# An FFN's gate and up by seven half-token products of block sums instead of eight, in a one-core Conformer-style block

## The reference

```python
def swiglu(h, w_gate, w_up, w_down):
    return (jax.nn.silu(h @ w_gate) * (h @ w_up)) @ w_down

x = x + 0.5 * swiglu(rms_norm(x, ffn1_norm), ffn1_w_gate, ffn1_w_up, ffn1_w_down)
h = rms_norm(x, mix_norm)
proj = h @ w_in                        # 1024 x 4624
...                                    # SSD scan of 16 heads, pooling over 4 groups
x = x + concatenate([y_ssd, y_pool]) @ w_out
x = x + 0.5 * swiglu(rms_norm(x, ffn2_norm), ffn2_w_gate, ffn2_w_up, ffn2_w_down)
out = rms_norm(x, final_norm)
```

## Time and profile before

| | us |
|---|---|
| median of 3 runs | 1042.38 |
| lowest, highest | 1042.3, 1042.4 |
| the profiled execution, device time | 1042.32 |
| its span in the trace | 1040.6 |
| busy: TensorE, VectorE, ScalarE, GpSimd | 1031.2, 559.6, 380.4, 179.1 |

### The profile page before, as it was taken

How to read it: one execution, slowest core, us unless ns; L and a number is a source line. 1 busy time by engine, 2 the same in 40 slices (tenths; PEclk the granted TensorE clock), 3 DMA queues, 4 the chain that set the end, 5 groups by cost and what they waited for, 6 DMA issues and landing times.

```text
span 1040.6 us, 13577 instructions
## 1 busy us (share of the span) xinstructions
PE 1031.2 (99%) x4798; PEld 847.3 (81%) x4798; DVE 559.6 (54%) x686; ACT 380.4 (37%) x489; POOL 179.1 (17%) x166
## 2 busy tenths in 40 slices
PE   9999999999999999999999999999999999999997
PEld 7888888888888878878787888888888888888887
DVE  5544444444344468786799795554444444433432
ACT  6433223322333337652234753432333223332332
POOL 1110110101001032221063451110101101101100
PEclk9999999999999999999999999999999999999998
DMA  6533323322333343222222233333333332233222
GB/s 184 150 113 101 101 86 95 101 83 68 99 98 96 101 124 100 82 81 70 73 81 81 62 101 101 101 101 90 92 101 101 96 87 89 79 109 95 86 68 81
DMA packets 188873, 99.09 MB, mean 95 GB/s; under 512 B 3780, under 2 KB 188200, under 8 KB 188840
## 3 DMA queue, kind: packets, MB, share of 16 engines
q1 hardware_dynamic: 188168, 97.60, 32.3%
q10 hardware_dynamic: 672, 1.05, 0.3%
HBM read 96.54 MB, written 2.10 MB: 95 GB/s over the span
## 4 chain that ended last, share of the span: by engine, by line
PE 96%; DVE 3%; issue 1%; ACT 1%; POOL 0%; ACTq 0%; POOLq 0%
PE bank L1150 29%; PE bank L1152 29%; PE bank L1151 29%; PE bank L1222 1%; PE bank L1216 1%; PE bank L1219 1%; PE bank L1471 1%; PE bank L1284 0%; PE bank L1306 0%; PE bank L1472 0%; PE bank L1473 0%; PE bank L1274 0%; DVE w_lo_part L743 0%; DVE ebuf L903 0%; PE bank L1190 0%
## 5 line engine op out<-in xcount | busy, mean ns | idle before, releaser
L1150 PE MATMUL bank<-xghi,w_hi_part 128*128 128x512 f32 x960 | 377.4, 393 | 0.0
L1152 PE MATMUL bank<-xghi,w_lo_part 128*128 128x512 f32 x960 | 373.8, 389 | 0.0
L1151 PE MATMUL bank<-xglo,w_hi_part 128*128 128x512 f32 x960 | 373.6, 389 | 0.0
L743 DVE TENSOR_TENSOR w_lo_part<-w_raw,w_hi_part 128x1024 fp32r<-128x1024 f32 x194 | 253.9, 1309 | 192.8 <-ACT w_hi_part L498 187.5
L498 ACT ACTIVATE w_hi_part<-w_raw 128x1024 fp32r<-128x1024 f32 x194 | 203.8, 1051 | 196.2 <-PE bank L1152 194.7
L1150 PEld LDWEIGHTS bank<-xghi,w_hi_part 128*128 128x128 f32 x960 | 180.2, 188 | 39.9 <-issue 2.8
L1151 PEld LDWEIGHTS bank<-xglo,w_hi_part 128*128 128x128 f32 x960 | 180.3, 188 | 38.4 <-issue 1.2
L1152 PEld LDWEIGHTS bank<-xghi,w_lo_part 128*128 128x128 f32 x960 | 180.2, 188 | 37.5
L1150 PE MATMUL bank<-acthi,w_hi_part 128*128 128x512 f32 x330 | 130.5, 396 | 0.0
L410 POOL TENSOR_TENSOR gate_buf<-gate_buf,rstd 128x512 f32<-128x512 f32 x44 | 57.1, 1298 | 424.5 <-ACT gate_buf L521 424.5
L1152 PE MATMUL bank<-acthi,w_lo_part 128*128 128x512 f32 x330 | 129.4, 392 | 0.0
(11 more groups left out here) (223 smaller groups left out, 805.0 us busy)
## 6 DMA issues: line engine op xcount, KB each, us to landing
w_raw<-in_ffn_w_gate SPq DMA_DIRECT2D x42, 512.0 KB, 3.8
w_raw<-in_ffn_w_up SPq DMA_DIRECT2D x42, 512.0 KB, 3.8
w_raw<-in_w_in SPq DMA_DIRECT2D x29, 512.0 KB, 3.8
w_raw<-in_ffn_w_down SPq DMA_DIRECT2D x32, 384.0 KB, 3.2
w_raw<-in_ffn_w_down SPq DMA_DIRECT2D x32, 320.0 KB, 3.0
w_raw<-in_w_out SPq DMA_DIRECT2D x16, 512.0 KB, 3.6
out<-xtok SPq DMA_DIRECT2D x4, 512.0 KB, 3.4
xload<-in_x SPq DMA_DIRECT2D x3, 512.0 KB, 7.0
```

The lines of the kernel that those rows point to most:

```text
L743: dve.tensor_tensor(wlo[:, slot(m)], raw[:, slot(m)], whi[:, slot(m)].bitcast(F32), ALU.subtract).then_inc(w_lo, 1)
L1150: pe.matmul(bank, w, h, start=first and n == 0, stop=False)
L1151: pe.matmul(bank, w, l, start=False, stop=False)
L1152: mm = pe.matmul(bank, wl, h, start=False, stop=last and n == blocks - 1)
```

## The change

Two hidden tiles of gate and up are taken together as a quad. With k for the two halves of the 1024 input channels, f for the two tiles, and the 512 tokens in two halves, gate and up are each a 2 x 2 by 2 x 2 block product. Instead of its eight block products the kernel makes seven, of sums of blocks (`A11`, `SUM1`, `SUM2`, `A12`, `SUM3`, `SUM4`, `A22`); each has 4 input blocks, gate and up, three matmuls: 24 matmuls of 256 columns. Some accumulate onto an earlier product in the same bank, the rest is added by VectorE (`gather`) after ScalarE has copied a product out of PSUM.

- Sums of weights: three by VectorE, one by GpSimd per quad. There are 7 conversions per quad where there were 4, all of 1024 elements.
- Sums of x (`combine`): four 256-token combinations for each of the 4 channel pairs, split into `thi` and `tlo`, once per FFN; in FFN1 in the steps of direct tiles 2 and 3, in FFN2 in the last four out-projection units.
- Direct, as before: tiles 0 to 3 of FFN1, tiles 0 and 1 of FFN2. So 9 and 10 quads.
- Each FFN runs in three groups of 8, 8 and 6 tiles; after each group all 8 output tiles get that group's part of down. `acthi`, `actlo` hold 8 tiles instead of 22. The first two down items of a group begin with all tiles but the last two.
- Up is not scaled by `rstd` any more; half of `rstd` is multiplied onto the down result (`down_scaled`), and a second VectorE instruction adds it to x.
- Eight raw buffers instead of four within FFNs; the loops are written out.

```diff
-DOWN = (6, 6, 5, 5)
+RAW = 8
+KH = UB // 2
+GROUP_TILES = (8, 8, 6)
+DIRECT_TILES = (4, 2)
+PARTS = 7
+A11, SUM1, SUM2, A12, SUM3, SUM4, A22 = range(PARTS)
...
 @blk.sync
+                if FREE[key]:
+                    sp.wait_ge(w_lo, FREE[key])
+                if key[0] == 1 and slot >= RING:
+                    sp.wait_ge(unit_done, M_FFN2)
...
 @blk.gpsimd
+            def third_sum(q):
+                pool.wait_ge(sum_ready[1], q + 1)
+                pool.tensor_tensor(weight(q, SUM3), weight(q, A11), weight(q, SUM3), ALU.add).then_inc(sum_ready[3], 1)
+            def scale_gate(q, i, h, done, ready):
+                pool.wait_ge(done, q + 1)
+                gate = post[:, q % 2, i, 0:HALF]
+                pool.tensor_tensor(gate, gate, rstd[:, half(h)], ALU.mult).then_inc(ready, 1)
             def gates(f):
+                        if not quad.chained:
+                            third_sum(q)
+                        scale_gate(q, 0, 0, c11_done, r11_ready)
+                        if not quad.last:
+                            third_sum(q + 1)
+                        scale_gate(q, 1, 1, c22_done, r22_ready)
+                        scale_gate(q, 2, 1, c12_done, r12_ready)
...
 @blk.scalar
+            def ffn(f, last):
+                for r, it in enumerate(items):
+                    if it.kind == "product" and it.part == SUM1:
+                        copy_product(q, A11, 0, q % 2, p1_read, act0_ready)
+                    if it.kind == "product" and it.part == SUM2:
+                        copy_product(q, SUM1, 1, 2, p5_read, act22_ready)
+                    if it.kind == "product" and it.part == A12:
+                        copy_product(q, SUM2, 2, q % 2, u2_read, act0_ready)
+                    if chained and it.part == SUM1:
+                        silu_odd(q - 1)
+                    if before is not None and before.kind == "direct":
+                        direct_post(f, before)
+                    if converted <= n + 3 < M_FFN2 + len(FFN2):
+                        convert(n + 3)
+                    if chained and it.part == A11:
+                        silu_even(q - 1)
+                    if chained and it.part == SUM2:
+                        split_act(q - 1, 0)
+                    if chained and it.part == SUM3:
+                        split_act(q - 1, 1)
+                    if f == 0 and it.kind == "direct" and it.raw >= RING:
+                        halves_of_x(0, it.raw - RING, R_N1)
+                        combination_hi(0, it.raw - RING)
+                    if it.kind == "down" and it.d == 0:
+                        silu_even(q)
+                        silu_odd(q)
+                        split_act(q, 0)
+                        split_act(q, 1)
+                    if it.kind == "down" and it.group == 2 and it.d:
+                        last(it.d - 1)
...
+            for d in range(DK):
+                square(2, d, d % 2, xT[:, cols(d)])
+                norm_hi(2, d, R_N2)
+                if d >= KH:
+                    halves_of_x(1, d - KH, R_N2)
+                    combination_hi(1, d - KH)
+                convert(M + U_OUTS + d + RING)
...
 @blk.vector
+            def combine(f, j, gain):
+                term(0, low[:, 0:HALF], g0, b12[:, j, :], ALU.subtract)
+                term(2, high[:, HALF:S], g4, b12[:, j, :], ALU.subtract)
+                dve.wait_ge(t_own, c + 1)
+                term(1, high[:, HALF:S], neg4, t32[:, j, 0, :], ALU.subtract)
+                dve.wait_ge(t_own, c + 3)
+                term(3, high[:, 0:HALF], neg4, t32[:, j, 1, :], ALU.subtract)
+            def combine_low(f, j):
+                dve.wait_ge(t_hi, KH * f + j + 1)
+                dve.tensor_tensor(tlo[:, :, j, :], t32[:, j, :, :], thi[:, :, j, :].bitcast(F32),
+                                  ALU.subtract).then_inc(t_lo, 1)
+            def first_sum(q):
+                dve.tensor_tensor(weight(q, SUM1), weight(q, SUM3), weight(q, A22), ALU.add).then_inc(sum_ready[1], 1)
+            def gather(q, part, i, bank, read, ready):
+                dve.wait_ge(unit_done, QUADS[q].base + part + 1)
+                dve.wait_ge(read, q + 1)
+                c = post[:, q % 2, i, :]
+                dve.tensor_tensor(c, c, PB[bank][:, :], ALU.add).then_inc(ready, 1)
+            def down_scaled(f, g, d, rows=slice(0, S), bank=None):
+                dve.scalar_tensor_tensor(out=upd[:, d % 2, rows], in0=bank if bank is not None else PB[4 + d % 2][:, :],
+                                         scalar=0.5, in1=rstd[:, rows], op0=ALU.mult,
+                                         op1=ALU.mult).then_inc(d_read, 1)
+            def ffn(f, last):
+                for r, it in enumerate(items):
+                    if chained and it.part == A11:
+                        gate21(q - 1)
+                    if it.kind == "down" and it.d == 0:
+                        gate21(q)
+                    if product and it.part == SUM1:
+                        fourth_sum(q)
+                    if product and it.part == SUM3:
+                        gather(q, A12, 0, 3, p1_read, c11_done)
+                    if product and it.part == SUM4:
+                        gather(q, SUM3, 1, q % 2, p5_read, c22_done)
+                    if product and it.part == A22:
+                        gather(q, SUM4, 2, 2, u2_read, c12_done)
+                    if before is not None and before.kind == "direct":
+                        direct_post(f, before, n - 1)
+                    if before is not None and before.kind == "down":
+                        update(f, before.group, before.d, last)
+                    if starts_quad(n + 3):
+                        first_sum(ffn_item(n + 3).quad)
+                    if starts_quad(n + 2):
+                        second_sum(ffn_item(n + 2).quad)
+                    if converted <= n + 2 < M_FFN2 + len(FFN2):
+                        convert(n + 2)
+                    if before is not None and before.kind == "direct" and before.part:
+                        act_low(f, before.tile, before.tile % 2)
+                    if f == 0 and it.kind == "direct" and it.raw >= RING:
+                        combine(0, it.raw - RING, R_N1)
+                        combine_low(0, it.raw - RING)
+                    if chained and it.part == SUM1:
+                        act_even(q - 1)
+                    if chained and it.part == SUM2:
+                        act_low(f, QUADS[q - 1].tile, 0)
+                        act21(q - 1)
+                    if chained and it.part == A12:
+                        act22(q - 1)
+                    if chained and it.part == A22:
+                        act_low(f, QUADS[q - 1].tile + 1, 1)
...
+            ffn(0, last1)
+            update(0, 2, DK - 1, last1)
+            for m in (M_MIX + 2, M_MIX + 3):
+                convert(m)
...
+            for d in range(DK):
+                dve.wait_ge(unit_done, d + (M + U_OUTS + 1))
+                dve.tensor_tensor(xT[:, cols(d)], PB[4 + d % 2][:, :], xT[:, cols(d)], ALU.add).then_inc(x_ready, 1)
+                norm_lo(2, d, R_N2)
+                if d >= KH:
+                    combine(1, d - KH, R_N2)
+                convert(M + U_OUTS + d + RING)
+                if d >= KH:
+                    combine_low(1, d - KH)
...
 @blk.tensor
+            def product(f, it, n):
+                if part == A11 and local >= 2:
+                    pe.wait_ge(act21_ready, q - 1)
+                if part == SUM2:
+                    pe.wait_ge(p1_read, q + 1)
+                if part == SUM3:
+                    pe.wait_ge(u2_read, q + 1)
+                if part == SUM4:
+                    pe.wait_ge(p5_read, q + 1)
+                if part == A22:
+                    pe.wait_ge(c22_done, q + 1)
+                pe.wait_ge(w_hi, n + 1)
+                pe.wait_ge(w_lo, n + 1)
+                for e in range(2):
+                    out = bank[:, half(e)]
+                    for k in range(KH):
+                        if part == SUM1 and local == 0 and e == 0:
+                            pe.wait_ge(t_lo, KH * f + k + 1)
+                        pe.matmul(out, w, hi, start=opens and e == 0 and k == 0, stop=False, skip_group_check=True)
+                        pe.matmul(out, w, lo, start=False, stop=False, skip_group_check=True)
+                        mm = pe.matmul(out, wl, hi, start=False, stop=end, skip_group_check=True)
```

More of the change, by code:

```diff
@@ L70, with ffn_item, starts_quad, raw_uses @@
 M_FFN2 = M_MIX + U_OUTS + DK
-N_UNITS = M_FFN2 + N_GU + N_DOWN
+FFN2 = ffn_items(1, M_FFN2)
+ITEMS = (FFN1, FFN2)
+START = (M_FFN1, M_FFN2)
+DIRECT_SEEN = (0, DIRECT_TILES[0])
+def ffn_item(n):
+    if n < M_MIX:
+        return FFN1[n - M_FFN1]
+    if M_FFN2 <= n < M_FFN2 + len(FFN2):
+        return FFN2[n - M_FFN2]
+    return None
+def starts_quad(n):
+    it = ffn_item(n)
+    return it is not None and it.kind == "product" and it.part == 0
+def raw_uses():
```

(31 more changed lines are left out.)

633 lines of the change are left out of this document (403 added, 230 removed).

## The result

The changed kernel takes 1060.07 us (median of 4 runs, 1058.46 to 1060.41); the kernel before, run beside it, 1042.34 us. The ratio is 1.0167, with a 95% interval of 1.015 to 1.0185. Forecast was 1020 us in a range to 1036: the sign is wrong.

The account below looks back on a forecast made before the run. TensorE, busy 99% of the span, was taken as the bound. Terms -51.8 + 11.7 + 3 + 11 + 1.5 + 2.6 = -22.0 us took the 1042.4 us median to 1020; own range 1010 to 1031, with rivals (a) and (b) 1001 to 1036.

Parts of the forecast that it names:

- the term of the matmuls: Gate and up, nineteen quads: 1824 matmuls at 0.2267 us go, 3192 at 0.1133 come, -51.8 us.
- rival (b): Quad matmuls run in the slow mode, 0.118 us each, and waits shrink: 1026 us; chance 0.12.
- the estimate of 98 ns: Spacing of 256-column matmuls, on a straight line between the skill's 81 ns at 128 columns and 131 at 512.
- End of FFN1: Update's second instruction in the path, 0.7, and two mixer conversions ahead of the reciprocal: +1.5 us.
- FFN1's first quad: Combinations of x in FFN1's direct steps 4 to 7 make SUM1 wait: +3 us (0 to 6).
- The pause: TensorE waits 0.9 us before A11 on 13 chained quads, GpSimd's third sum ahead of the second: +11.7 us.
- The start of FFN2: Combinations in the last four out-projection tiles make FFN2's first product wait for x's low part: +11 us (5 to 14).
- Rival (c): VectorE with GpSimd bounds each chained quad, 22.2 us, about 1050 us; decides from 21.6 a quad; chance 0.09.
- (a): TensorE stays the bound, GpSimd's turns fall into gaps, combinations cost half: about 1000 us; chance 0.22.
- (d): Weight loads not hidden behind half a matmul, 188 ns each set the pace: about 1230 us; chance 0.01.
- Group ends: Activations after A22 need about 4.3 us, partial downs put 5.5 to 8.2 in front: cost 0 (to +3).
- the tail: End of the kernel: last tiles have 18 matmuls rather than 66, exposing scaling, add and transposes: +2.6 us (1 to 5).

Follow-up runs that it names:

- run 512: Not a follow-up run: in "they run 512 columns" the word is a verb, for gate and up matmuls of 512 columns in the kernel before.

## Why the prediction was wrong

**The failed step** is the term of the matmuls: "gate and up run in the quick one, so I take 0.1133". It is 18.8 us too good (3192 x 0.0059). The quad matmuls gave back 33.0 us and not 51.8. The stretch of 64 distances at 0.1133 in the earlier trace rows was taken as the rule and the 17 at 0.118 as the exception, although the rule rested on one stretch at the very end of the kernel. With halving alone, 0.120 is the lasting price in gate and up, while that same stretch keeps its 0.1133. The other end, kept as rival (b), was nearer and still too low. That gate and up would run halves in the quick mode because they run 512 columns in it was an assumption, and no row showed it. What makes the difference of 0.0067 stays open. It moves with the width of the weights (0.1156 with 64 columns in two of three) and with the cut (0.287 for the uneven pair), but the downs at 0.2333 have the same surplus where a load of 188 ns has 227 ns to hide in.

The Trainium skill (TensorE: Matmul & The Clock Gate, Back-to-back issue gap) says that load and matmul together set the sustained spacing; the runs here agree in kind (0.287 for 384 and 128 columns). Its numbers, and the estimate of 98 ns made from them, aren't those of this kernel. The same page of the Trainium skill (LDWEIGHTS) lets the time of a load go with its columns, 107 ns for 128. The recorded loads agree with the slope, 188 ns for 128 columns and 134 for 64, but not with the length.

**The second miss** is at the ends of stages. With the true price the forecast would have been about 1039, still below the kernel before, and with the waits as measured but the matmuls at 0.1133 the time would have been 1060 - 18.8 = 1041. So the sign needed both misses. The other 21 us, net of the shorter pauses, lie here and in the 512-column matmuls (5.0, a term that I did not have).
- End of FFN1: 11.1 for 1.5. I priced one instruction and the reciprocal, and did not walk the list of eight down units of 4.1 us. Two VectorE instructions, a wait for ScalarE, a low part and a conversion make 5.2. For FFN2's start the same walk was made, and it held: it had tile 7's low part 32 us behind tile 4's end, that is 679.06 - 16.35 + 32 = 694.7; TensorE's wait for it ended at 694.40.
- FFN1's first quad: 9.9 for 3. The steps were summed, without VectorE's wait of 1.12 for ScalarE's copy and without the slow matmuls.
- Clock: no term had it. In the changed kernel, behind each of the waits of 2.8 to 8.5 us, matmuls ran at the 1.2 GHz level: about 32 in FFN1's first quad (3.0 us), and the first ones of the mixer and behind FFN2's wait. These waits thus cost a quarter to a half more than their length. A wait of 2.6 us at the start of FFN2, in the kernel with the out-projection's order changed, left the granted clock at 1.00; the same wait in the kernel with the third sum moved was followed by matmuls 0.43 apart.

**What was right.** The pause is where the walk had it: before A11, at 13 places, with the third sum in front of the second. It is 0.37 for 0.9 us, mostly because A11 is wanted at 3 x 2.86 = 8.6 and not at 8.16. The start of FFN2 is 13.0 for 11. Rival (c) did not decide: 20.4 us a chained quad, below 21.6, so the slower time came by another way than that rival. Rivals (a) and (d) fell; TensorE wasn't paced by 188 ns. Group ends (2.2 for 0) and the tail (4.0 for 2.6) were short.

## What to carry over

Don't price a matmul that gets shorter by its columns: halve it in the old kernel, in the stage where it will run, and time that alone before you count on the saving. A stretch elsewhere in the kernel can have another price. Walk each engine's list wherever the unit of the faster engine gets shorter (down units of 4.1 us, tiles with extra terms), also where the edit adds but one instruction; a wait for another engine counts in the list as much as an instruction. Put work that waits for another engine behind work that doesn't: three such moves gave back 19.6 us without removing any work.

## What the runs showed of the hardware

- A float32r matmul with 128 x 128 weights costs 0.2267 us at 512 columns in gate and up. Cut in two, it costs 0.120 a half there, and a pair of 384 and 128 costs 0.287; with 64 weight columns in two of three, the halves cost 0.1156 in the mean.
- Cutting gate and up in halves took the untouched 512-column downs of FFN1 from 0.229 to 0.2333, the same 0.0067 above 0.2267 as 0.120 above 0.1133; in the changed kernel they are at 0.233 too. With narrower loads or the uneven cut they stayed at 0.229. The last output tile ran 64 distances at 0.1133 in the kernel before and with the halves. Why isn't known; the granted clock was 1.00 throughout.
- After idling 8.5 us TensorE ran its next 512-column matmuls 0.43 apart, at a granted clock of 0.50 (1.2 GHz); after idling 3.4 and 2.8 us it ran 256 columns 0.21 apart, at 0.50.
- An add of 1024 elements with both operands in SBUF takes VectorE 1.22 us with GpSimd idle and 2.83 where GpSimd's own add (L542) is running when it starts; that one takes 3.40. Begun 0.17 us ahead of a GpSimd scaling (853.37), the VectorE add still takes 1.22, and the scaling 1.65.
